# Weights of the first modulation loaded and summed by feature halves, the first slab of w_in ahead of them, ScalarE making the first four chunks

## The chip, the cores and the metric

One core of one Trainium2 chip. The time is device microseconds (us) of one execution of the whole program, the median of several runs. All times below that are not durations count from the start of the profiled span.

## The reference, cut to what matters

The program computes two transformer blocks on 512 tokens of 1024 features in float32. The change lies in the first 50 us, which compute the modulation and the first normalised, modulated input:

```python
mod = c @ w_ada[l] + b_ada[l]                 # c: (1, 1024), w_ada: (1024, 6144)
sh1, sc1, gt1, sh2, sc2, gt2 = jnp.split(mod, N_MOD, axis=-1)
h = modulate(rms_norm(x, g_pre_mix[l]), sh1, sc1)      # h * (1 + sc1) + sh1
proj = h @ w_in[l]                            # w_in: (1024, 5120)
```

All that follows (short convolution, stick-breaking attention, MLP, the second block) is untouched.

## The kernel before, in words

Features lie on the partitions: the 1024 features are 8 chunks (DC) of 128, the 512 tokens 4 row tiles (NT). A float32 product is made of three matmuls of split operands (`mm3`, L910 to L913): high part by high part, high by low, low by high. I call one such group of three a product of TensorE. Weights come as slabs of 2048 floats a partition (4 chunks by 512 columns, 1 MB) into a ring of three, `w_raw`. GpSimd splits each slab: `w_hi` (L757, for slab 0 L765), then `w_lo` = raw minus high (L759; for slab 0 four pieces, L769). The activations of chunk c are split too: ScalarE copies `ht_hi` (L1652, L1654), VectorE subtracts to `ht_lo` (L2202, recorded at L2050).

**The queue of SP.** All large loads go through one queue in the order of the program text: 16 blocks of w_ada (512 KB each, `ada`, L602, one chunk of 128 input features by the 1024 columns of shift for blocks 0 to 7 and of scale for 8 to 15), the four rows of x behind blocks 5, 7, 9 and 11 (X_WITH), then slab 0 of w_in, a wait for all 16 sums (L614), slab 1, slab 2, four blocks of w_ada for the next columns, and from there one slab and four blocks in turn. A block waits until the buffer of the block seven before it is free, a slab from slab 3 on until TensorE has begun the slab two before it (`slab_free`).

**VectorE** multiplies each block by a column of c and adds it to `ada_acc` (`ada_product`, L2144 on; recorded at L2059 for the first of a column and L2054 for the others). Between the products it makes the reciprocals of the row norms (NORM_WITH, L2072) and, behind block 11, copies the small vectors (VEC_WITH, L2183).

**TensorE** transposes each normalised row of x into six banks (`first_rows`, L1139), sums `ada_acc` over the partitions by matmuls with a column of ones (`first_sums`, L1113: for s = 0 the shift, for s = 1 the scale; a bank holds shift and scale of four chunks and is full after the fourth and eighth column of s = 1), transposes chunks 6 and 7 into the two banks that `first_mod` has emptied, and then starts `features`. For slab 0 this works by pieces: chunk `new` is awaited, and all products that it completes are done, 1 + 3 + 5 + 7 = 16 (L935 to L941).

**Behind the sums:** `first_mod` (VectorE, three operations of 4 columns a half), then pairs of chunks: VectorE scales and shifts the even chunk in PSUM (`first_affine`, L2061), ScalarE the odd one (L1650), ScalarE makes both high parts, VectorE both low parts. Then VectorE goes on with the products of the third and fourth column of w_ada, the convolution of the first branch, the fifth column, and the gating, whose results free banks and so let TensorE go on.

## Time and profile before

| | us |
|---|---|
| median of 3 runs (range) | 1486.69 (1484.39 to 1486.77) |
| the profiled execution | 1484.37 |
| its span | 1482.6 |
| TensorE matmul busy | 1440.1 |
| VectorE busy | 851.4 |
| GpSimd busy | 990.2 |
| ScalarE busy | 552.9 |

Durations and moments come from the one profiled execution; what lies around its span is 1.8 us. PE is TensorE's matmul, PEld its weight load, DVE VectorE, ACT ScalarE, POOL GpSimd, SP the engine that issues most DMAs (SPq its queue). Matmuls are pipelined, so that a row can show 0.39 us where the next matmul starts 0.23 us later. Where the profile shows a small operation x16, it can be eight float32 matmuls in two passes each.

### The profile page before, as it was taken

The page shows a single profiled execution, that of the slowest core. Times are in us where ns is not written, and L with a number is a line of the kernel's source. Part 1 is how long each engine was busy: PE and PEld are TensorE (multiplying, and loading weights), DVE is VectorE, ACT ScalarE, POOL GpSimd, SP SyncE. Part 2 cuts the span into 40 slices and gives each one's busy share as a digit, 9 for nine tenths or more (in the row PEclk, how much of TensorE's full clock was granted, in tenths as well). Part 3 has the DMA queues.
Part 4 walks back from the last instruction along what each step waited for, and adds up shares of the span by engine and source line. Part 5 has one row for each costly group of instructions (what it writes and reads, how often), then busy time and mean ns, then how long its engine had stood idle before and what let it go on. Part 6 is the DMA issues. An engine that isn't in the chain of part 4 may idle for free.

```text
span 1482.6 us, 18612 instructions
## 1 busy us (share of the span) xinstructions
PE 1440.1 (97%) x6987; PEld 1169.7 (79%) x6987; DVE 851.4 (57%) x1334; ACT 552.9 (37%) x1075; POOL 990.2 (67%) x400
## 2 busy tenths in 40 slices
PE   3999999999999999999999999999999999999997
PEld 3888877778898888888898844789789888888886
DVE  6998156554565555666744786441516555465655
ACT  3201133433454344444333376452424523333214
POOL 1857554355668899888568996365153989788653
PEclk9999999999999999999999999999999999999999
DMA  9875321223543332322443200133024323232131
GB/s 349 298 270 209 100 85 57 86 86 106 169 153 114 114 113 87 114 86 85 156 126 109 86 1 1 59 125 123 7 86 142 114 86 114 86 114 86 57 97 74
DMA packets 103385, 167.88 MB, mean 113 GB/s; under 512 B 3917, under 2 KB 61185, under 8 KB 102785
## 3 DMA queue, kind: packets, MB, share of 16 engines
q1 hardware_dynamic: 100176, 160.45, 31.7%
q10 hardware_dynamic: 3121, 6.26, 1.4%
q8 instruction: 56, 0.92, 0.2%
q14 instruction: 32, 0.26, 0.1%
HBM read 161.97 MB, written 4.72 MB: 112 GB/s over the span
## 4 chain that ended last, share of the span: by engine, by line
PE 84%; DVE 10%; ACT 3%; DMA 2%; issue 1%; POOL 1%; DVEq 0%; SPq 0%; ACTq 0%; POOLq 0%
PE bank L911 25%; PE bank L913 25%; PE bank L912 25%; DVE bank L2054 2%; DMA ada_w<-in_w_ada 1%; DVE smx L2507 1%; DVE x L2050 1%; PE bank L1372 1%; PE bank L1429 1%; PE bank L1448 1%; DVE bank L2050 1%; PE bank L1183 1%; DVE m L2050 1%; ACT junk L1541 1%; PE bank L1195 1%
## 5 line engine op out<-in xcount | busy, mean ns | idle before, releaser
L911 PE MATMUL bank<-ht_hi,w_hi 128*128 128x512 f32 (+1 forms) x1200 | 442.9, 369 | 0.5 <-DVE ht_lo L2050 0.3
L912 PE MATMUL bank<-ht_hi,w_lo 128*128 128x512 f32 (+1 forms) x1200 | 440.1, 367 | 0.0
L913 PE MATMUL bank<-ht_lo,w_hi 128*128 128x512 f32 (+1 forms) x1200 | 440.0, 367 | 0.0
L759 POOL TENSOR_TENSOR w_lo<-w_raw,w_hi 128x2048 fp32r<-128x2048 f32 x83 | 389.8, 4697 | 6.9
L757 POOL TENSOR_SCALAR w_hi<-w_raw 128x2048 fp32r<-128x2048 f32 x83 | 162.3, 1955 | 343.5 <-DMA w_raw<-in_w_in 111.2
L911 PEld LDWEIGHTS bank<-ht_hi,w_hi 128*128 128x128 f32 x1200 | 226.5, 189 | 41.6 <-issue 2.7
L913 PEld LDWEIGHTS bank<-ht_lo,w_hi 128*128 128x128 f32 x1200 | 226.6, 189 | 37.1
L912 PEld LDWEIGHTS bank<-ht_hi,w_lo 128*128 128x128 f32 x1200 | 226.6, 189 | 36.8 <-issue 0.5
L809 POOL TENSOR_TENSOR dn_lo<-dn_raw,dn_hi_all 128x1024 fp32r<-128x1024 f32 x77 | 184.6, 2418 | 56.7 <-ACT dn_hi_all L1738 56.6
L2054 DVE SCALAR_TENSOR_TENSOR uc<-bank,par,uc 128x511 f32<-128x511 f32 x88 | 66.0, 750 | 128.7 <-ACT uc L1992 125.6
L823 POOL TENSOR_TENSOR dn_raw<-dn_raw 128x1024 f32<-128x1024 f32 x44 | 105.8, 2404 | 12.8 <-PE bank L913 4.8
L911 PE MATMUL bank<-w_hi,ht_hi 128*128 128x512 f32 x256 | 100.4, 392 | 0.2 <-DVE facc L2050 0.2
L1992 ACT ACTIVATE uc<-bank,par 128x512 f32<-128x512 f32 x44 | 34.4, 781 | 176.9 <-PE bank L913 176.7
L913 PE MATMUL bank<-w_lo,ht_hi 128*128 128x512 f32 x256 | 99.7, 389 | 0.0
L912 PE MATMUL bank<-w_hi,ht_lo 128*128 128x512 f32 x256 | 99.6, 389 | 0.0
L2050 DVE TENSOR_TENSOR facc<-bank,facc 128x512 f32<-128x512 f32 x120 | 83.0, 692 | 22.4 <-PE bank L913 14.3
L2054 DVE SCALAR_TENSOR_TENSOR ada_acc<-ada_w,cvec,ada_acc 128x1024 f32<-128x1024 f32 x42 | 85.2, 2028 | 8.0 <-DMA ada_w<-in_w_ada 4.2
L1738 ACT CAST dn_hi_all<-dn_raw 128x1024 fp32r<-128x1024 f32 x77 | 77.1, 1054 | 18.4 <-PE bank L913 15.2
L2050 DVE TENSOR_TENSOR bank<-bank,hr 128x512 f32<-128x512 f32 x32 | 22.4, 700 | 82.9 <-ACT hr L1751 82.3
L911 PE MATMUL bank<-dn_hi_all,hf_hi 128*128 128x512 f32 x176 | 68.6, 390 | 0.4 <-POOL dn_lo L809 0.4
L912 PE MATMUL bank<-dn_hi_all,hf_lo 128*128 128x512 f32 x176 | 68.5, 389 | 0.0
L913 PE MATMUL bank<-dn_lo,hf_hi 128*128 128x512 f32 x176 | 68.5, 389 | 0.0
(305 smaller groups left out, 2415.7 us busy)
## 6 DMA issues: line engine op xcount, KB each, us to landing
w_raw<-in_w_in SPq DMA_DIRECT2D x27, 1024.0 KB, 5.0
ada_w<-in_w_ada SPq DMA_DIRECT2D x48, 512.0 KB, 7.3
w_raw<-in_w_up SPq DMA_DIRECT2D x22, 1024.0 KB, 5.0
w_raw<-in_w_mlp_in SPq DMA_DIRECT2D x16, 1024.0 KB, 5.5
dn_raw<-in_w_mlp_out SPq DMA_DIRECT2D x28, 512.0 KB, 4.8
w_raw<-in_w_out SPq DMA_DIRECT2D x8, 1024.0 KB, 5.0
w_raw<-in_w_mem_kv SPq DMA_DIRECT2D x8, 1024.0 KB, 5.2
dn_raw<-in_w_down SPq DMA_DIRECT2D x16, 512.0 KB, 4.7
```

Of the source, the lines that this page charges most:

```text
L757: g.tensor_scalar(w_hi[:, r], w_raw[:, r], 1.0, 1.0, ALU.mult, ALU.mult).then_inc(slab_hi, 1)
L759: g.tensor_tensor(w_lo[:, r], w_raw[:, r], w_hi[:, r].bitcast(F32), ALU.subtract).then_inc(slab_split, 1)
L809: g.tensor_tensor(dn_lo[:, w], dn_raw[:, w], dn_hi(w).bitcast(F32), ALU.subtract).then_inc(dn_split, 1)
L823: g.tensor_tensor(dn_raw[:, o], dn_raw[:, a], dn_raw[:, b], ALU.subtract).then_inc(t_made, 1)
L911: inc_free(pe.matmul(o, ah, bh, start=start, stop=False))
L912: pe.matmul(o, al, bh, start=False, stop=False)
L913: return pe.matmul(o, ah, bl, start=False, stop=stop)
L1183: ins = pe.transpose(t.ap[:, qt * P:qt * P + P], b1[:, j, O1[qt] + kc * P:O1[qt] + kc * P + P], ident[:])
L1738: st.done(act.copy(dn_hi(w), dn_raw[:, w]), dn_cast)
L1992: st.done(act.activation(uc[:, c], tiles[c].ap[:], ACT.Identity, scale=par[:, p, 2 + g, k:k + 1], bias=par[:, p, 6 + g, k:k + 1]), uc_ready)
L2050: do(v.tensor_tensor(o, a, b, op), sem, tile)
L2054: do(v.scalar_tensor_tensor(out=o, in0=a, scalar=s, in1=b, op0=op0, op1=op1), sem, tile)
```

## The change

The first 16 blocks of w_ada are cut otherwise. Block i below 8 now holds 512 columns of shift and the same 512 columns of scale (features 0 to 511) of input chunk i; blocks 8 to 15 hold the other 512 of both. So the first eight sums give shift and scale of chunks 0 to 3. Slab 0 goes ahead of all blocks, a row of x follows each of blocks 0 to 3, and the wait of the queue ahead of slab 1 is gone. The first sums are followed by slab 0's work at once; chunk 6's transposes, the second sums and chunk 7's transposes stand inside it (`within`). For chunks 0 to 3 ScalarE makes affine and high part alone; VectorE puts the products of blocks 8 to 15 around the first modulation and the low parts. Slab 1's high part is made by ScalarE, and its low part by GpSimd, behind a wait for all 16 sums.

```diff
@@ -43,9 +43,9 @@
 ADA_BUFS = 7
-X_WITH = (5, 7, 9, 11)
-NORM_WITH = (7, 9, 11, 13)
-VEC_WITH = 11
+X_WITH = (0, 1, 2, 3)
+NORM_WITH = (1, 2, 3, 4)
+VEC_WITH = 5
...
@@ -599,19 +599,23 @@
                 if i >= ADA_BUFS:
                     sp.wait_ge(ada_used, i - ADA_BUFS + 1)
                 s = i // DC
-                sp.dma_start(ada_w[:, r], wada[:, i % DC, s * D:(s + 1) * D]).then_inc(ada_loaded[r], 16)
-
+                if s < 2:
+                    sp.dma_start(ada_w[:, r].rearrange("p (j n) -> p j n", j=2),
+                                 wada[:, i % DC, 0:2 * D].rearrange("p (j n) -> p j n", j=2)[:, :, 512 * s:512 * s + 512]
+                                 ).then_inc(ada_loaded[r], 16)
+                else:
+                    sp.dma_start(ada_w[:, r], wada[:, i % DC, s * D:(s + 1) * D]).then_inc(ada_loaded[r], 16)
+
+            win = w_rows(A["w_in"])
+            load(raw4, win[:, 0:4, 512:1024])
             for i in range(2 * DC):
                 ada(i)
                 if i in X_WITH:
                     m = X_WITH.index(i)
                     sp.dma_start(x[:, m], A["x"][m * P:m * P + P, :]).then_inc(x_loaded[m], 16)
-            win = w_rows(A["w_in"])
             i = 2 * DC
             for c0 in (512, 1024, 0, 1536, 2048, 2560):
-                for s in range(2):
-                    if n == 1:
-                        sp.wait_ge(ada_used, 2 * DC)
+                for s in range(1 if c0 == 512 else 0, 2):
                     load(raw4, win[:, 4 * s:4 * s + 4, c0:c0 + 512])
                     for _ in range(4 if n > 2 else 0):
                         if i < 6 * DC:
@@ -755,13 +759,12 @@
                 g.wait_ge(slab_loaded[r], i * 16 + 16 * (n // RING + 1))
                 g.sem_inc(slab_go, 1)
                 g.tensor_scalar(w_hi[:, r], w_raw[:, r], 1.0, 1.0, ALU.mult, ALU.mult).then_inc(slab_hi, 1)
-                g.wait_ge(slab_hi, i * RING + n + 1 - (FF1_J - 2 if n >= S0["memkv2"] - 2 else 0))
+                g.wait_ge(slab_hi, i * RING + n - (FF1_J - 2 if n >= S0["memkv2"] - 2 else 0))
                 g.tensor_tensor(w_lo[:, r], w_raw[:, r], w_hi[:, r].bitcast(F32), ALU.subtract).then_inc(slab_split, 1)
 
             def split_first():
 
                 g.wait_ge(slab_loaded[0], 16)
-                g.wait_ge(ada_used, 2 * DC)
                 g.tensor_scalar(w_hi[:, 0], w_raw[:, 0], 1.0, 1.0, ALU.mult, ALU.mult).then_inc(slab_hi, 1)
                 g.wait_ge(slab_hi, 1)
                 raw, hi, lo = (w[:, 0].rearrange("p (k n) -> p k n", k=4) for w in (w_raw, w_hi, w_lo))
@@ -800,7 +803,9 @@
             taps = conv31()
             n = S0["w_in2"] + 6
             split_first()
-            split(1)
+            g.wait_ge(second_hi, 1)
+            g.wait_ge(ada_used, 2 * DC)
+            g.tensor_tensor(w_lo[:, 1], w_raw[:, 1], w_hi[:, 1].bitcast(F32), ALU.subtract).then_inc(slab_split, 1)
             split_all(2, S0["mlp"])
 
             def split_down(u, w):
...
@@ -936,7 +942,9 @@
                             each(new)
                             Tile(t0 + new).wait_free(pe)
                             pe.wait_ge(first_lo if new < 3 else slab_split, new + 1 if new < 3 else 1)
-                            for m, k in [(m, new) for m in range(new)] + [(new, k) for k in range(new + 1)]:
+                            for at, (m, k) in enumerate([(m, new) for m in range(new)] + [(new, k) for k in range(new + 1)]):
+                                if (new, at) in within:
+                                    within[new, at]()
                                 c = slice(m * P, m * P + P)
                                 mm3(Tile(t0 + m).ap[:, 0:n], wh[:, k, c], wl[:, k, c], ah[:, k], al[:, k], k == 0, False)
                         state["owed"] += 1
@@ -1106,13 +1114,13 @@
 
                 pe.wait_ge(ada_used, DC * (s + 1))
                 for c in range(DC):
-                    t = Tile(T0["ada01"] + c // 4)
-                    if s == 0 and c % 4 == 0:
+                    t = Tile(T0["ada01"] + s)
+                    if c == 0:
                         t.wait_free(pe)
-                    at = DC * s + c
+                    at = DC * (c // 4) + 4 * s + c % 4
                     ins = pe.matmul(t.ap[:, at:at + 1], ada_acc[:, s, c * P:c * P + P], ones[:, 0:1], start=True,
                                     stop=True)
-                    if s == 1 and c % 4 == 3:
+                    if c == DC - 1:
                         ins.then_inc(t.full, 1)
 
             def modulation(s):
@@ -1143,14 +1151,16 @@
             for m in range(NT):
                 if m == 1:
                     turn_rows()
-                if m == NT - 1:
-                    first_sums(0)
                 first_rows(range(DC - 2), m)
-            first_sums(1)
-            for c in (DC - 2, DC - 1):
+            first_sums(0)
+
+            def first_chunk(c):
                 for m in range(NT):
                     first_rows((c,), m)
-            features(T0["w_in"], 2, ht_hi, ht_lo, each=lambda k: Tile(NT1_T[k]).wait_taken(pe), first=True)
+
+            features(T0["w_in"], 2, ht_hi, ht_lo, each=lambda k: Tile(NT1_T[k]).wait_taken(pe), first=True,
+                     within={(1, 0): lambda: first_chunk(DC - 2), (3, 3): lambda: first_sums(1),
+                             (3, 6): lambda: first_chunk(DC - 1)})
             for c in range(1, 5):
                 features(T0["w_in"] + 4 * c, 2, ht_hi, ht_lo)
             tokens(T0["w_in"] + 20, 2, ht_hi, ht_lo)
@@ -1641,14 +1651,25 @@
                 norm_stat("nt1", m, x[:, m])
                 act.wait_ge(norm_inv, NB["nt1"] + m + 1)
                 st.done(act.activation(xn1[:, m], x[:, m], ACT.Copy, scale=stat[:, 16 + m:17 + m]), xn_ready)
-            for pair in range(DC // 2):
+            def first_affine(c):
+                t = Tile(NT1_T[c])
+                t.wait_full(act)
+                st.done(act.activation(t.ap[:], t.ap[:], ACT.Identity, scale=mod[:, 1, c:c + 1], bias=mod[:, 0, c:c + 1]))
+
+            Tile(T0["ada01"]).wait_taken(act)
+            for c in range(4):
+                first_affine(c)
+                act.wait_ge(act_step, st.value(act_step))
+                st.done(act.copy(ht_hi[:, c], Tile(NT1_T[c]).ap[:]), nt1_hi)
+            act.wait_ge(slab_loaded[1], 16)
+            st.done(act.copy(w_hi[:, 1], w_raw[:, 1]), second_hi)
+            for pair in range(DC // 4, DC // 2):
                 c = 2 * pair + 1
                 if pair % 2 == 0:
                     Tile(T0["ada01"] + pair // 2).wait_taken(act)
                 t = Tile(NT1_T[c])
-                t.wait_full(act)
-                st.done(act.activation(t.ap[:], t.ap[:], ACT.Identity, scale=mod[:, 1, c:c + 1], bias=mod[:, 0, c:c + 1]))
-                act.wait_ge(nt1_affine, pair + 1)
+                first_affine(c)
+                act.wait_ge(nt1_affine, pair - DC // 4 + 1)
                 st.done(act.copy(ht_hi[:, c - 1], Tile(NT1_T[c - 1]).ap[:]), nt1_hi)
                 act.wait_ge(act_step, st.value(act_step))
                 st.done(act.copy(ht_hi[:, c], t.ap[:]), nt1_hi)
@@ -2172,7 +2193,7 @@
                         if j % 2:
                             stt(mod[:, j], mod[:, j], 1.0, col((V_G1, V_GM1)[j // 2], 8), ALU.add, ALU.mult)
 
-            for i in range(2 * DC):
+            for i in range(DC):
                 ada_product(i)
                 if i in NORM_WITH:
                     norm_inv_of("nt1", NORM_WITH.index(i))
@@ -2201,13 +2222,17 @@
                 v.wait_ge(nt1_hi, c + 1)
                 tt(ht_lo[:, c], t.ap[:], ht_hi[:, c].bitcast(F32), ALU.subtract, tile=t)
 
+            for i in range(DC, DC + 2):
+                ada_product(i)
             first_mod(0)
-            first_affine(0)
+            for c in range(4):
+                ada_product(DC + 2 + c)
+                first_low(c)
+            for i in range(DC + 6, 2 * DC):
+                ada_product(i)
             first_mod(1)
-            first_low(0)
-            first_affine(2)
-            first_low(1)
-            for pair in range(1, DC // 2):
+            first_affine(4)
+            for pair in range(2, DC // 2):
                 if pair + 1 < DC // 2:
                     first_affine(2 * pair + 2)
                 first_low(2 * pair)
```

## Rows read from the trace of the kernel before

**Rows 1.** The page, parts 1 and 2: busy time; granted clock in 40 slices

```profile
PE 1440.1 (97%) x6987; PEld 1169.7 (79%) x6987; DVE 851.4 (57%) x1334; ACT 552.9 (37%) x1075; POOL 990.2 (67%) x400
...
PEclk9999999999999999999999999999999999999999
```

**Rows 2.** List of waits of PE, whole run: total us, times, longest

```profile
PE bank L1139 <- ACT xn L1643: 19.9, 3, 15.7
...
PE bank L1183 <- DVE b L2050: 3.2, 1, 3.2
```

**Rows 3.** Timeline, DVE, 0 to 34: start, us, operation, idle before

```profile
4.37 0.75 DVE L2059 TENSOR_SCALAR ada_acc<-ada_w,cvec 128x1024 f32<-128x1024 f32 x1 [0.95 <-DMA ada_w<-in_w_ada]
...
14.68 1.28 DVE L2054 SCALAR_TENSOR_TENSOR ada_acc<-ada_w,cvec,ada_acc 128x1024 f32<-128x1024 f32 x1 [1.56 <-DMA ada_w<-in_w_ada]
...
19.21 0.75 DVE L2059 TENSOR_SCALAR ada_acc<-ada_w,cvec 128x1024 f32<-128x1024 f32 x1 [1.51 <-DMA ada_w<-in_w_ada]
...
22.76 2.67 DVE L2054 SCALAR_TENSOR_TENSOR ada_acc<-ada_w,cvec,ada_acc 128x1024 f32<-128x1024 f32 x2 [0.90 <-DMA ada_w<-in_w_ada]
...
25.80 0.60 DVE L2183 COPY vec<-bank 128x428 f32<-128x428 f32 x1
...
29.77 2.67 DVE L2054 SCALAR_TENSOR_TENSOR ada_acc<-ada_w,cvec,ada_acc 128x1024 f32<-128x1024 f32 x2
```

**Rows 4.** Timeline, PE, 30 to 51

```profile
32.86 3.41 PE L1113 MATMUL bank<-ones,ada_acc 128*128 128x1 f32 x16
...
36.13 1.97 PE L1139 MATMUL bank<-ident,xn 128*128 128x128 f32 x8
...
37.77 0.77 PE L911 MATMUL bank<-ht_hi,w_hi 128*128 128x512 f32 x1
...
39.49 0.77 PE L911 MATMUL bank<-ht_hi,w_hi 128*128 128x512 f32 x1
...
50.17 0.39 PE L911 MATMUL bank<-ht_hi,w_hi 128*128 128x512 f32 x1
```

**Rows 5.** Timeline, POOL, 30 to 60

```profile
32.77 1.90 POOL L765 TENSOR_SCALAR w_hi<-w_raw 128x2048 fp32r<-128x2048 f32 x1 [30.24 <-DMA w_raw<-in_w_in]
...
34.75 4.98 POOL L769 TENSOR_TENSOR w_lo<-w_raw,w_hi 128x512 fp32r<-128x512 f32 x4
...
41.69 4.62 POOL L759 TENSOR_TENSOR w_lo<-w_raw,w_hi 128x2048 fp32r<-128x2048 f32 x1
...
55.79 1.92 POOL L757 TENSOR_SCALAR w_hi<-w_raw 128x2048 fp32r<-128x2048 f32 x1 [2.59 <-DMA w_raw<-in_w_in]
```

**Rows 6.** Busy time by stretches: engines, clock, share of DMA, GB/s

```profile
15.00:20.00 5.00, 1.06 (x5) 1.07 (x6) 3.17 (x4) 2.17 (x3) 0.00 (x0) 1.00 1.03 405
...
35.00:40.00 5.00, 4.89 (x18) 3.87 (x19) 3.75 (x9) 3.85 (x7) 5.00 (x5) 1.00 1.05 412
```

**Rows 7.** Timeline, ACT, 12 to 36

```profile
13.19 1.06 ACT L1541 ACTIVATE junk<-x 128x1024 bf16<-128x1024 f32 x1 [4.06 <-DMA x<-in_x]
...
14.37 0.29 ACT L1543 ACTIVATE stat<-stat,eps_t 128x1 f32<-128x1 f32 x1
...
17.74 1.15 ACT L1643 ACTIVATE xn<-x,stat 128x1024 f32<-128x1024 f32 x1 [3.07 <-DVE stat L2065]
...
35.20 0.75 ACT L1650 ACTIVATE bank<-bank,mod 128x512 f32<-128x512 f32 x1 [4.35 <-DVE mod L2050]
```

**Rows 8.** Timeline, DVE, 46 to 55

```profile
46.56 2.19 DVE L2059 TENSOR_SCALAR ada_acc<-ada_w,cvec 128x1024 f32<-128x1024 f32 x1
...
48.85 5.43 DVE L2054 SCALAR_TENSOR_TENSOR ada_acc<-ada_w,cvec,ada_acc 128x1024 f32<-128x1024 f32 x1
```

**Rows 9.** Timeline, PE, around 171

```profile
171.56 3.63 PE L1129 MATMUL bank<-ones,ada_acc 128*128 128x1 f32 x32
```

**Rows 10.** Timeline, SP and POOL, 106 to 123: slab 8

```profile
106.76 0.43 SPq L588 DMA_DIRECT2D w_raw<-in_w_in  x1
...
116.55 5.46 POOL L759 TENSOR_TENSOR w_lo<-w_raw,w_hi 128x2048 fp32r<-128x2048 f32 x1
```

More of the change, by code:

```diff
@@ L455, in build @@
         slab_hi, slab_split, slab_free = sem("slab_hi"), sem("slab_split"), sem("slab_free")
-        slab_go, first_lo = sem("slab_go"), sem("first_lo")
+        slab_go, first_lo, second_hi = sem("slab_go"), sem("first_lo"), sem("second_hi")
         c_loaded, rows_loaded, mem_loaded = sem("c_loaded"), sem("rows_loaded"), sem("mem_loaded")
@@ L920, in all_taken, with features @@
                     Tile(t).wait_taken(pe)
-            def features(t0, ks, ah, al, i=None, tper=0, sper=0, n=T, each=None, first=False, behind=None):
+            def features(t0, ks, ah, al, i=None, tper=0, sper=0, n=T, each=None, first=False, behind=None,
+                         within={}):
                 for s in range(ks):
```

## The prediction

> **What bounds the kernel now.** The page comes first: TensorE is busy 97% of the span and nothing else is over 80% [rows 1]. The list of PE waits over the whole run says where the other 3% lies: 19.9 us wait for the normalised rows at the very start, and the next wait is 3.2 us [rows 2]. So whatever lets TensorE enter its dense part earlier comes off the end one for one, as long as nobody is late behind it. The timeline of the first 51 us is where the change is decided. VectorE sums sixteen 512 KB blocks of w_ada as they land, the last ending at 29.77 + 2.67 = 32.44 [rows 3]; TensorE turns the sums (until 36.3), and its first weight product starts at 37.77 [rows 4]. The sixteen products of slab 0 (three matmuls each) end at 50.17, where slab 1 begins [rows 4]. I call 50.17 the entry: from there TensorE runs at 0.68 us a product, 10.9 us a slab. The sum below is the new entry against 50.17.
>
> **When the first half is summed.** The queue now carries slab 0, then a block of w_ada and a row of x in turn, then blocks only. Counting places of 512 KB, the rows tell when a place is usable: place 1 at 4.37, 8 at 14.68, 11 at 19.21, 14 at 22.76 [rows 3], slab 0 (places 21 and 22) at 32.77 [rows 5]. The new order puts slab 0 at 5.8, block 0 (place 3) at 7.2, block 1 at 10.2, 2 at 13.2, 3 at 16.2, 4 at 19.2, 5 at 20.4, 6 at 21.6, 7 (place 14) at 22.8. The new w_ada blocks consist of 2 KB runs instead of 4 KB. The trace has both kinds: 405 GB/s in 15:20 with 4 KB runs, 412 GB/s in 35:40 with the slabs' 2 KB runs [rows 6]. I charge nothing.
>
> VectorE also makes four reciprocals and the copy of vec. A row of x costs ScalarE 1.47 (13.19 to 14.66) for the deviation, then 0.2 for the reciprocal and 1.15 for the scaling [rows 7], about 3.0 a row. From x at 8.8 the reciprocals fall at 11.7, 14.7, 17.7 and 20.7, each within 0.4 us behind a product that is ready; so product 5 runs 20.9 to 22.2, vec and mod_g take 0.9 (25.80 to 26.7 [rows 3]), product 7 ends at 25.8, two at 1.34 each. The data alone would allow 24.1.
>
> GpSimd's split of slab 0 moves from 32.77 to 5.8, beside products 0 and 1; it takes 1.9 + 4.98 in four pieces [rows 5]. A product that takes 1.28 alone [rows 3] took 5.43 beside a 2048-wide w_lo [rows 8], so a piece of 1.25 can hold one by at most its own length: 0 to 1.3, twice at most. I take 0.5: first half summed at 26.3. The Trainium skill (SBUF — State Buffer, Who interferes with whom) says that a VectorE instruction with two SBUF inputs and a GpSimd one that reads SBUF exclude each other for a whole instruction. The 5.43 agrees with it; by the rule product 1 waits for one piece, a delay between 0 and 1.25, which would not change the forecast.
>
> **When TensorE starts.** Before, 5.33 us passed from the last product to the first matmul (32.44 to 37.77). The chain is kept (sums, three small VectorE operations, affine 0.75 [rows 7], copy, difference), but the first tile is now full after all eight columns instead of four of the second eight: half of 3.41, +1.7 [rows 4]. ScalarE did the odd chunks' affines before, at 0.75 [rows 7], as fast as VectorE, so its doing chunk 0's costs nothing. Start: 26.3 + 5.3 + 1.7 = 33.3, which is 4.4 earlier.
>
> **What TensorE now does behind the start.** Slab 0 took 12.4 from start to entry and needs it again. New inside it:
> - The second half's sums. The same sixteen instructions took 3.41 at the start [rows 4], but 32 of them took 3.63 at 171 us [rows 9], so 1.8 if TensorE runs at its full pace by then. It has twelve products behind it: I take 1.8.
> - The transposes of chunks 6 and 7, before ahead of the start: 1.97 for eight at the slow pace [rows 4], about 1.05 at the fast one. I take 1.5.
> - VectorE puts a product (1.34) between two differences (0.7), so chunk 1 is ready 2.1 behind the start, where the first product took 1.6: 0.5.
> - The slow pace at the start (first product 1.6, second 1.16, then 0.68) lasts a little longer with that pause and the transposes in it: 0 to 3 (six products at 1.16), I take 0.5.
> - The second half's chunks: from the end of its sums, modulation 0.8, two affines 1.8, copies and four differences take about 6.0 until chunk 7 is taken; TensorE has four products, chunk 7's transposes and three products of slab 1 to do, 5.4. A wait of 0.5.
>
> VectorE reaches product 15 at about 42.4 (30.9, six products, four differences), ahead of TensorE's twelfth product at 44.5, so the sums don't wait. Slab 1's w_lo waits behind it on GpSimd, to 47: ahead of the entry. ScalarE's w_hi of slab 1 (about 2, twice its 1024-wide operations) falls into its idle time around 37. Entry: 33.3 + 12.4 + 1.8 + 1.5 + 0.5 + 0.5 + 0.5 = 50.5, against 50.2: **0.3 us later**. The head start of 4.4 is spent on 4.8 of work that formerly stood before the start or lay in waits.
>
> **Behind the entry.** VectorE starts the third column's products at about 52.8 instead of 46.56. But before, its first two took 7.7 us, to 54.3, beside slab 2's split (2.19 and 5.43 [rows 8]); now that split passes beside operations that read PSUM, and the two take 2.2, to 55.0. The next must begin before slab 3's w_hi (55.79 [rows 5]); it does by 0.8. If not, VectorE is a product behind until a w_lo of 5.46 [rows 10] falls on the last of the fourth column, and everything behind it is up to 5.5 late. There is cover: slab 8 is issued at 106.76, held back by product 32, and split at 122.0 [rows 10]; TensorE wants it at 50.2 + 7 x 10.88 = 126.3. The cover is 4.3, so this costs 0 to 1.2. On SP, slab 1 and 2 no longer wait for the sixteenth sum (32.4) and nothing stands behind that wait.
>
> **The time.** The profiled execution took 1484.37 for a span of 1482.6; with +0.3 it is 1484.7. The median of the runs is 1486.69, 2.3 above that execution, so the forecast is 1487.0.
>
> **Rivals.**
> 1. *The head start is kept.* If VectorE follows the data (24.1 instead of 26.3) and TensorE is fast from its second product, the entry is 50.5 - 2.2 - 1.0 - 0.5 = 46.8, or 3.4 earlier: 1483.3. For it: the reciprocals lag by only tenths each. Against it: ScalarE's 3.0 a row is as long as two places of the queue, so there is no slack to catch up.
> 2. *TensorE stays at its slow pace through slab 0.* The first matmuls took 0.77 where later ones take 0.39, though the granted clock stands at 1.00 throughout, the 2.4 GHz level [rows 1, 4]. The slow stretch followed a stretch of transposes and one-column sums. If the pause behind chunk 0 and chunk 6's transposes extend it by six products (+3.0, less the 0.5 counted) and the sums fall into it (+1.6), with the transposes at 2.0 (+0.5), the entry is 4.6 later than mine, 4.9 later than before: 1491.6. It decides from about five slow products on (+2.7 over before). For it: TensorE now has gaps in just this stretch. Against: before, it was fast 2.9 us behind 37.77. The Trainium skill (TensorE: Matmul & The Clock Gate, What you observe) says that the clock doubles only after sustained matmuls; by it the first products run at 1.2 GHz. The durations agree, the granted-clock column doesn't show it, and the price above is from rows.
> 3. *VectorE slips a product behind.* Condition and price above: +0.3 and up to 1.2, 1488.2. Near a coin's edge (0.8 us), but within what is told apart.
> 4. *The change does nothing*: were the entry set by slab 1's split. It isn't: slab 1 was split at 46.3 before [rows 5], 3.9 ahead.
>
> **Chances.** Forecast 0.44, rival 3 0.16, rival 1 0.20, rival 2 0.16, others 0.04. A measurement here tells 0.2% (3.0 us) from no change. Forecast and rival 3 lie within it; rival 1 is just beyond it, and half of the rest goes to either side: faster 0.22, same 0.60, slower 0.18. The range goes from 1482.8 (a little beyond rival 1, for 0.5 less delay by GpSimd) to 1490.5 (rival 2 with four slow products instead of six).
>
> **What would show it.** First weight product at 33.3 (32 to 34.5); slab 1's first matmul at 50 to 51; product 7 ending near 26; the second sums at half their old duration; PE wait of some 0.5 in front of chunk 6 or 7 of slab 1; product 18 starting ahead of slab 3's w_hi; no PE wait near 126. A first product after 35.5 or an entry before 48 would prove me wrong.

## The result, and the profile after

The changed kernel takes 1487.88 us (median of 22 runs, 1486.13 to 1493.65); the kernel before, on the same chips, 1485.24 (22 runs). The ratio is 1.0021, 95% interval [1.0013, 1.0028]: 3.1 us slower, 1.9 to 4.2. The profiled execution of the changed kernel took 1493.65 and is one of its longest (four of the 22 lie above 1491.8, the others between 1486 and 1490); experiment 12 has the profile of an execution near the usual time.

The page after, and the list of PE waits over the whole run (columns as in [rows 1] and [rows 2]):

```profile
PE 1442.8 (97%) x6987; PEld 1168.7 (78%) x6987; DVE 846.6 (57%) x1332; ACT 555.7 (37%) x1078; POOL 986.6 (66%) x399
```

```profile
PE bank L1147 <- ACT xn L1653: 12.0, 3, 10.4
PE bank L916 <- DVE yt_lo L2071: 6.4, 1, 6.4
...
PE bank L1193 <- DVE b L2071: 3.3, 1, 3.3
```

The start did what it was to do: the wait for the normalised rows fell from 19.9 to 12.0. In its place stands a wait of 6.4 for yt_lo, which the kernel before doesn't have. The timeline of VectorE, as [rows 3, 8]:

```profile
23.76 2.67 DVE L2075 SCALAR_TENSOR_TENSOR ada_acc<-ada_w,cvec,ada_acc 128x1024 f32<-128x1024 f32 x2
...
51.80 2.23 DVE L2080 TENSOR_SCALAR ada_acc<-ada_w,cvec 128x1024 f32<-128x1024 f32 x1
54.12 4.06 DVE L2075 SCALAR_TENSOR_TENSOR ada_acc<-ada_w,cvec,ada_acc 128x1024 f32<-128x1024 f32 x3
61.35 7.44 DVE L2075 SCALAR_TENSOR_TENSOR ada_acc<-ada_w,cvec,ada_acc 128x1024 f32<-128x1024 f32 x2 [3.17 <-DMA ada_w<-in_w_ada]
...
99.33 0.70 DVE L2071 TENSOR_TENSOR bank<-bank,cv 128x512 f32<-128x512 f32 x1
...
112.91 15.49 DVE L2075 SCALAR_TENSOR_TENSOR ada_acc<-ada_w,cvec,ada_acc 128x1024 f32<-128x1024 f32 x7
...
131.72 2.28 DVE L2071 TENSOR_TENSOR yt_lo<-bank,yt_hi 128x512 fp32r<-128x512 f32 x3
```

The kernel before has at the same places:

```profile
91.89 0.70 DVE L2050 TENSOR_TENSOR bank<-bank,cv 128x512 f32<-128x512 f32 x1
...
106.46 11.07 DVE L2054 SCALAR_TENSOR_TENSOR ada_acc<-ada_w,cvec,ada_acc 128x1024 f32<-128x1024 f32 x7
...
120.86 3.08 DVE L2050 TENSOR_TENSOR yt_lo<-bank,yt_hi 128x512 fp32r<-128x512 f32 x4
```

The timeline of PE, as [rows 4]:

```profile
26.48 3.58 PE L1121 MATMUL bank<-ones,ada_acc 128*128 128x1 f32 x16 [2.36 <-DVE ada_acc L2075]
32.94 0.77 PE L916 MATMUL bank<-ht_hi,w_hi 128*128 128x512 f32 x1 [2.88 <-DVE ht_lo L2071]
...
35.13 1.09 PE L1147 MATMUL bank<-ident,xn 128*128 128x128 f32 x4 [0.56 <-DVE ht_lo L2071]
...
43.78 1.84 PE L1121 MATMUL bank<-ones,ada_acc 128*128 128x1 f32 x16
...
47.66 0.60 PE L1147 MATMUL bank<-ident,xn 128*128 128x128 f32 x4
...
49.45 0.47 PE L916 MATMUL bank<-ht_hi,w_hi 128*128 128x512 f32 x1 [0.49 <-DVE ht_lo L2071]
```

The product that starts at 49.45 is slab 1's first: 0.7 ahead of 50.17 [rows 4] (0.35 ahead by the end of slab 1's first tile, read from the first copy of cv: 52.74 after, 53.09 before). So up to here the change is neutral or a little better. Now ScalarE's own DMA queue, SP's issue of slabs 3 and 8, and GpSimd, as [rows 5, 10]:

```profile
49.38 0.36 ACTq L1541 DMA_DIRECT2D ada_b<-in_b_ada  x1
...
49.77 0.45 ACTq L1678 DMA_DIRECT2D gpost<-in_g_post_mix  x1
50.25 0.45 ACTq L1678 DMA_DIRECT2D gpost<-in_g_post_mlp  x1
```

```profile
49.95 0.38 SPq L588 DMA_DIRECT2D w_raw<-in_w_in  x1
...
113.21 0.43 SPq L588 DMA_DIRECT2D w_raw<-in_w_in  x1
```

```profile
60.26 1.91 POOL L761 TENSOR_SCALAR w_hi<-w_raw 128x2048 fp32r<-128x2048 f32 x1 [6.79 <-DMA w_raw<-in_w_in]
...
119.90 1.93 POOL L761 TENSOR_SCALAR w_hi<-w_raw 128x2048 fp32r<-128x2048 f32 x1 [14.22 <-DMA w_raw<-in_w_in]
121.91 5.42 POOL L763 TENSOR_TENSOR w_lo<-w_raw,w_hi 128x2048 fp32r<-128x2048 f32 x1
```

Slab 3 of the kernel before, for comparison, from SP's timeline (its w_hi is in [rows 5]):

```profile
50.59 0.38 SPq L588 DMA_DIRECT2D w_raw<-in_w_in  x1
```

ScalarE issues three loads of 512 KB (ada_b, gpost twice) behind its last copy of chunk 7. Before, they went out at 43.31 to 44.18 and had landed when slab 3 was asked for; now they go out at 49.38 to 50.25, around slab 3 (49.95). Slab 3 is usable 10.3 us behind its issue, before 5.2 (50.59 to 55.79), and the blocks behind it are late too: VectorE idles 3.17 for block 20. VectorE reaches the gating of the convolution at 99.33, before at 91.89: 7.4 late. Product 32 then comes 7.4 late as well, slab 8 is issued at 113.21 instead of 106.76 [rows 10], and one of the seven products behind it is caught by slab 8's w_lo (15.49 for seven; before 11.07). The end of this chain in TensorE's window (columns as in [rows 6]) and in ScalarE's timeline:

```profile
125.00:140.00 15.00, 8.59 (x33) 6.67 (x32) 13.64 (x14) 4.30 (x8) 9.60 (x3) 0.77 0.59 212
```

```profile
147.89 0.59 ACT L1645 COPY k<-bank 128x512 f32<-128x512 f32 x1 [13.70 <-PE bank L918]
```

And before:

```profile
125.00:140.00 15.00, 15.00 (x68) 12.43 (x67) 14.37 (x7) 0.59 (x1) 10.47 (x3) 1.00 0.42 129
```

```profile
140.13 0.59 ACT L1635 COPY k<-bank 128x512 f32<-128x512 f32 x1 [13.01 <-PE bank L913]
```

TensorE is busy 8.59 of 15 us where it was busy all 15 before, and the granted clock averages 0.77 (before 1.00). The first copy of k was at 140.13 before: 7.8 of the 9.3 us by which this span is longer are lost here, the other 1.5 at 180:190, where the clock stands at 0.84 and 0.82.

### The profile page after: what moved, and what is told of

Read it like the earlier page. It is cut to its first block, busy times and chain, and to the rows that moved or that the text cites. A ratio compares the mean times of both kernels' runs of the same rounds, so it can differ in the third digit from the quotient of the medians.

```text
span 1491.9 us, 18610 instructions
## 1 busy us (share of the span) xinstructions
PE 1442.8 (97%) x6987; PEld 1168.7 (78%) x6987; DVE 846.6 (57%) x1332; ACT 555.7 (37%) x1078; POOL 986.6 (66%) x399
## 4 chain that ended last, share of the span: by engine, by line
PE 79%; DVE 14%; ACT 3%; DMA 1%; issue 1%; DVEq 0%; SPq 0%; ACTq 0%
PE bank L916 24%; PE bank L917 23%; PE bank L918 23%; DVE ada_acc L2075 4%; DVE bank L2075 2%; DMA ada_w<-in_w_ada 1%; DVE bank L2071 1%; DVE smx L2532 1%; DVE x L2071 1%; PE bank L1382 1%; PE bank L1439 1%; PE bank L1458 1%; ACT junk L1551 1%; DVE m L2071 1%; PE bank L1205 1%
## 5 line engine op out<-in xcount | busy, mean ns | idle before, releaser
L763 POOL TENSOR_TENSOR w_lo<-w_raw,w_hi 128x2048 fp32r<-128x2048 f32 x82 | 382.6, 4665 | 6.8
```

What stands on the lines that cost most here:

```text
L763: g.tensor_tensor(w_lo[:, r], w_raw[:, r], w_hi[:, r].bitcast(F32), ALU.subtract).then_inc(slab_split, 1)
```

## Experiments

Each ran on one chip together with the kernel before, whose median there was 1484.65 for experiments 1 to 4, 1484.63 for 5 to 8, 1486.42 for 9 to 11 and 1484.27 for 12. The ratio is always to this kernel before. Median against median says less here than the ratio and the profile, since the kernel before itself has two levels, about 1484 and about 1487 (see experiments 5 and 9). A profile shows one execution, and where that is not a usual one the text says so.

**1. ScalarE's three loads early (in the changed kernel).**

```
     st.done(act.copy(w_hi[:, 1], w_raw[:, 1]), second_hi)
+    load_ada_b(0, 2)
+    for j, name in enumerate(("g_post_mix", "g_post_mlp")): act.dma_start(gpost[:, j], ...)
...  # behind chunk 7's copy:
-    load_ada_b(0, 2)
-    for j, name in ...
```

> The changed kernel, with ScalarE's three 512 KB loads (ada_b, two of gpost) issued behind its copy of slab 1's high part, near 38, instead of behind chunk 7, at 49.4 to 50.3. Theory 1 (collision): in the changed kernel these loads stood in the DMA engines together with slab 3 and blocks 20 to 23 (slab 3 took 10.3 us from issue to use instead of 5.2), and that alone put VectorE behind; with them gone the wait for yt_lo (6.4) falls to nothing, slab 8 is issued near 107, and the time is 0.3 to 0.8 us under the kernel before (ratio 0.9995 to 1.0). Theory 2 (late start): VectorE begins the third column 5.2 us later than before (51.8 against 46.56), and that puts it behind whatever the DMA does; then the wait stays at 4 us or more and the ratio at 1.002.

1486.41 (12 runs), ratio to before 1.0002 [0.9993, 1.0011]. GpSimd's and VectorE's timelines:

```profile
55.04 2.08 POOL L761 TENSOR_SCALAR w_hi<-w_raw 128x2048 fp32r<-128x2048 f32 x1 [1.64 <-DMA w_raw<-in_w_in]
```

```profile
51.77 2.19 DVE L2080 TENSOR_SCALAR ada_acc<-ada_w,cvec 128x1024 f32<-128x1024 f32 x1
54.06 20.86 DVE L2075 SCALAR_TENSOR_TENSOR ada_acc<-ada_w,cvec,ada_acc 128x1024 f32<-128x1024 f32 x7
...
96.98 0.70 DVE L2071 TENSOR_TENSOR bank<-bank,cv 128x512 f32<-128x512 f32 x1
```

The loads went out at 35.42 to 36.29. Slab 3 is usable 5.1 behind its issue (49.92) again, the wait for yt_lo is gone, and k is copied at 140.11. With this one edit the ratio falls from 1.0021 to 1.0002: the loss came from where the loads went. The profile is of the shortest of the 12 executions (1484.04). VectorE is still 5.1 late at the convolution (96.98), and slab 8 is issued at 110.86, 4.1 late: that costs nothing.

**2. The kernel before, its loads held back.** The same meeting made without any of the change.

```
+    act.wait_ge(slab_free, 1)      # TensorE has left slab 0
     load_ada_b(0, 2)
```

> The kernel before, with ScalarE waiting until TensorE has begun slab 1 (slab_free at 1, near 50.3) before it issues the same three loads. Theory 1: slab 3 lands some 4 to 5 us later, VectorE waits for block 20, reaches the convolution some 5 us late, and the first yt_lo comes behind the moment at which TensorE wants its bank (126): a PE wait of 1 to 6 us and a ratio of 1.0007 to 1.004. Theory 2: VectorE starts on time, so the third column has the same lead as before; no PE wait near 126 and a ratio of 1.000.

1488.09 (11 runs), ratio 1.0015 [1.0006, 1.0024]. Its PE waits and GpSimd's timeline:

```profile
PE bank L911 <- DVE yt_lo L2051: 6.4, 1, 6.4
```

```profile
60.07 1.92 POOL L757 TENSOR_SCALAR w_hi<-w_raw 128x2048 fp32r<-128x2048 f32 x1 [7.21 <-DMA w_raw<-in_w_in]
```

One wait in the old kernel reproduces the late slab (issued 50.79, usable 60.07), and in the profiled execution the wait of 6.4 and the late k copy (148.71) too. That execution is the longest of the 11 (1492.94, the others 1486.56 to 1488.88), so the wait of 6.4 is shown for it alone; the loss of the others is seen in the ratio. With experiment 1 this shows the cause from both sides.

**3. Slab 0 behind block 7 (on top of experiment 1).**

```
-    load(raw4, win[:, 0:4, 512:1024])      # ahead of block 0
+    if i == 7: load(raw4, win[:, 0:4, 512:1024])
```

> The first kernel of this series (loads early) with slab 0 behind block 7 in the queue instead of ahead of block 0. Everything up to the first half's sums comes two places (2.7 us) earlier: product 7 ends near 23.8 instead of 26.4, the first weight product starts near 30.3 instead of 32.9, slab 1's first matmul near 47 instead of 49.4, since VectorE's products 8 to 15 also move. Slab 0's split then lies beside products 7 to 9. If the head start is spent inside slab 0 whatever it is, as TensorE's own work, this gives 2 to 2.7 us against the first kernel of the series: ratio to before near 0.998. If the data of blocks 8 to 15 (same place as before) bound the second half, it gives under 1 us.

1486.96 (12 runs), ratio 1.0015 [1.0002, 1.0028]. VectorE's timeline:

```profile
19.75 0.16 DVE L2087 RECIPROCAL stat<-stat 128x1 f32<-128x1 f32 x1 [1.40 <-ACT stat L1554]
...
22.33 4.11 DVE L2076 SCALAR_TENSOR_TENSOR ada_acc<-ada_w,cvec,ada_acc 128x1024 f32<-128x1024 f32 x2
```

The blocks came earlier and nothing else did: VectorE waited 1.40 for ScalarE at each of the last three reciprocals, which are 2.95 apart (a row of x is ScalarE's bound), and products 6 and 7 took 4.11 instead of 2.67 beside slab 0's split. Product 7 ended at 26.44, as before the edit (26.37), and slab 1 began at 50.63, 1.2 later than in experiment 1 (49.42). The expectation that all would come 2.7 sooner fell.

**4. The gating ahead of three products of the fifth column (in the changed kernel).**

```
-    ada_products(4)
+    for c in range(5): ada_product(4 * DC + c)
     ...gating, yt_lo...
+    for c in range(5, DC): ada_product(4 * DC + c)
```

> The changed kernel, with VectorE doing the gating and yt_lo behind five products of the fifth column instead of behind all eight (the other three follow). If the bank that yt_lo frees is what TensorE waits for, the wait of 6.4 goes; what is late next is slab 8, issued at 113.2 and split at 127.3 against TensorE's 125.7, so 1.6 to 2 us of wait remain: 4 to 5 us less than the changed kernel where that one waits 6.4, and in the median a ratio of 1.000 to 1.0015. If it was slab 8 that TensorE waited for, nothing changes.

1492.12 (5 runs), ratio 1.0042 [1.0028, 1.0056]: worse, where 1.000 to 1.0015 had been expected. Its PE waits:

```profile
PE bank L916 <- POOL w_lo L763: 3.8, 1, 3.8
```

VectorE makes yt_lo from 121.53 on and k is copied at 140.37, so this wait can be moved away. But SP issues slab 10 only behind blocks that wait for those products: at 137.12, and TensorE waits 3.8 for its split. Behind this wait the granted clock stands at 0.87 and 0.79 over 150:160, so that more than the 3.8 is lost. It is the same lateness of VectorE, paid at its next customer.

**5. VectorE's order at the start (on top of 1).** From experiment 3: the fourth reciprocal and the copy of vec stand in front of products whose blocks are there.

```
-NORM_WITH = (1, 2, 3, 4); VEC_WITH = 5
+NORM_WITH = (1, 2, 3, 5); VEC_WITH = 7
```

> The changed kernel with ScalarE's three loads early (as in the first experiment) and VectorE's order at the start altered: the fourth reciprocal behind product 5 instead of product 4, and the copy of vec with mod_g behind product 7 instead of product 5. Theory A (the entry is set by VectorE's chain up to product 7, and the rest of the start follows it one for one): product 7 ends at 24.3 instead of 26.43 (it starts when its block has landed, about 23.0), first weight product at 30.8 instead of 32.9, slab 1's first matmul at 47.3 instead of 49.4, third column of VectorE at 49.7, no PE wait for yt_lo, k copy of the fifth column at 137.3 to 138; time 2.8 us below the kernel before. Theory B (the head start is spent again before the entry, on TensorE's slow first products and on waits for the second half's chunks): first weight product at 30.8, but slab 1's first matmul at 48.5 or later; time within 1.5 us of the kernel before. Theory C (the reciprocal put back delays ScalarE's last row so that its transposes hold the sums): first weight product not before 32.

1484.87 (11 runs), ratio 0.9995 [0.9987, 1.0004]. VectorE:

```profile
21.75 2.67 DVE L2075 SCALAR_TENSOR_TENSOR ada_acc<-ada_w,cvec,ada_acc 128x1024 f32<-128x1024 f32 x2
...
50.45 1.55 DVE L2080 TENSOR_SCALAR ada_acc<-ada_w,cvec 128x1024 f32<-128x1024 f32 x1
...
90.75 0.70 DVE L2071 TENSOR_TENSOR bank<-bank,cv 128x512 f32<-128x512 f32 x1
```

Product 7 ends at 24.42, the first weight product starts at 30.93, slab 1 at 48.10, the first k copy stands at 138.47: 1.7 ahead of before (the entry is 0.8 later than theory A had it: from start to entry 17.2 us passed, in the changed kernel 16.5; one cause is that the second and third product ran at the slow pace longer, full pace from 36.29, 5.4 behind the start, instead of 4.0). VectorE starts its third column 1.3 earlier than in experiment 1 and reaches the convolution 6.2 earlier: one product fewer is caught by a w_lo. Yet the span is 1482.8. The 1.7 is gone again, while the waits behind 146 us are those of the kernel before within 0.3 us each. The window rows (columns as in [rows 6]) tell:

```profile
170.00:175.00 5.00, 5.00 (x34) 4.69 (x33) 2.54 (x6) 0.00 (x0) 0.00 (x0) 0.75 0.27 104
175.00:180.00 5.00, 5.00 (x11) 2.83 (x10) 2.95 (x7) 0.00 (x0) 0.00 (x0) 0.57 0.09 19
```

TensorE counts as busy, but at a granted clock of 0.57. This begins within the 32 one-column sums (here 4.45, [rows 9] 3.63), and the stretch from SP's issue of slab 12 (the first of w_proj_conv, 146.85) to that of slab 14 (178.43) takes 31.6 where it takes 28.8 in the kernel before (148.51 to 177.28). That is a loss of 2.8, more than the 1.7. The rest comes back further on: the kernel before has a fall of its own at 225:235 (0.81 and 0.85), where TensorE has just waited 3.2 for VectorE's b (a tile of the attention); here the clock stays at 1.00 there, and from slab 14 to the next slab, issued near 291, it takes 112.8 instead of 113.7.

**6. The second sums behind 10 products instead of 12 (on top of 5).**

```
-within={..., (3, 3): first_sums(1), (3, 6): first_chunk(DC - 1)}
+within={..., (3, 1): first_sums(1), (3, 4): first_chunk(DC - 1)}
```

> The kernel before this one, and TensorE's second sums behind 10 of slab 0's 16 products instead of 12, chunk 7's transposes behind 13 instead of 15. Theory A: VectorE's product 15 ends ahead of the tenth product, so nobody waits for the sums; chunks 6 and 7 are ready 1.4 us earlier, the 0.5 us wait at slab 1 goes, VectorE's third column starts another 1.4 us earlier (48.3); time 0.5 us below the kernel before this one, 3.3 below the kernel before the change. Theory B: TensorE reaches the sums ahead of product 15 and waits 0.5 to 1.3 us, and the time is the same as without this edit or up to 1 us worse.

1484.45 (12 runs, three of them above 1488), ratio 0.9998 [0.9985, 1.0010]. The wait of 0.5 in front of slab 1 is gone, as theory A had it, but the profiled execution (1488.84, one of the three) lost 4.2 at yt_lo:

```profile
109.53 0.43 SPq L588 DMA_DIRECT2D w_raw<-in_w_in  x1
```

```profile
PE bank L916 <- DVE yt_lo L2071: 4.2, 1, 4.2
```

Slab 8 is issued 4.1 later than in experiment 5 (105.39) though VectorE started its third column 0.4 sooner (50.01): its first product was caught for 2.51 instead of 1.55 beside slab 2's split, and a product more fell behind a w_lo later. Neither theory had named this; it is the prediction's rival 3.

**7. The low parts of chunks 0 and 1 without a product between (on top of 6).** The edit: VectorE's product DC + 3 goes behind first_low(1) instead of in front of it.

> As the kernel before this one, and VectorE makes the low parts of chunks 0 and 1 one behind the other, with no product between. Theory A: TensorE's wait of 0.57 in front of chunk 1 goes and its products come to full pace sooner; slab 1's first matmul 0.5 earlier; product 15 at most 0.5 later, still ahead of the sums; time 0.5 us lower. Theory B: product 15 comes later than the tenth product, TensorE waits for the sums what it saved at chunk 1: no difference.

1484.81 (11 runs), ratio 0.9997 [0.9988, 1.0006]. Slab 1 starts at 47.17, 0.9 before experiment 5's and 3.0 before the old kernel's; the product is caught again (slab 8 issued at 109.56), TensorE waits 1.4 for slab 8's w_lo, and k is copied at 138.78. Then the clock falls to 0.57 in 175:180. Three us of head start brought nothing to the end.

**8. Experiment 6 with the loads where the change put them.**

> As e7 (start order and sums), but ScalarE's three loads stay behind its copy of chunk 7, where the change put them. The collision theory: the loads and slab 3 both move forward by about 2.5 us and still meet; slab 3's high part 9 to 11 us behind its issue instead of 5.2, VectorE waits 3 us or more for block 20 or its neighbours; but VectorE starts some 3 us earlier than in the changed kernel, so conv begins at 96 to 97, yt_lo comes in time, and the time is within 0.7 us of e7 in most executions. The rival (the meeting costs its 4 to 6 us whenever it happens, since VectorE's order has no slack anywhere): PE waits 3 to 6 us for yt_lo and the time is 2 us or more above e7.

1485.48 (12 runs, six at 1483.0 to 1483.9 and six at 1487.1 to 1494.6), ratio 1.0009 [0.9993, 1.0026]. The profile is of a short one (1482.0): slab 3, issued at 48.09, is usable at 57.03 (8.9 later), slab 8 is issued at 110.07, k copied at 139.29. So it is as the collision theory had it for half of the executions; the other half lies 4 to 11 us higher, and none of it was profiled.

**9. The kernel before, its sums taken apart.** The 32 one-column sums are 16 of column 3 and 16 of column 4; the four wide ones of column 2 go between.

```
-for s in range(2, 6): modulation(s)
+for s in (3, 2, 4, 5): modulation(s)
```

> The kernel before the change with one edit: behind the last column of the first stage TensorE makes the sums of w_ada in the order 3, 2, 4, 5 instead of 2, 3, 4, 5, so that its 32 one-column matmuls (3.6 us) are no longer in one piece but 16 and 16 with four wide ones (1.9 us) between. Theory D (the two levels in which the times of every kernel here lie, some 1484 and some 1487, are a drop of TensorE's granted clock behind these 32 sums: in the profiles of three kernels it stood at 0.57 in one 5 us window at 175:180 or 180:185 or near it and the stretch from slab 11 to slab 12 took 31.6 to 31.9 us, in the others at 1.00 and 28.8): with the sums apart nearly every execution is at 1484, the median falls to 1484.0 or below and none is above 1486. Rival D2 (the levels come from elsewhere, or it is not the sums' length that decides): the two levels stay with the same shares, median 1484.6 as before.

1484.05 (11 runs, 1482.98 to 1485.01) against 1486.42 for the kernel before on the same chip (29 runs, 18 of them above 1485.9): ratio 0.9985 [0.9977, 0.9994]. The upper level is gone. PE's timeline and the window:

```profile
169.90 1.84 PE L1129 MATMUL bank<-ones,ada_acc 128*128 128x1 f32 x16
171.60 1.96 PE L1126 MATMUL bank<-ada_acc,ones 128*128 128x512 f32 x4
173.40 1.84 PE L1129 MATMUL bank<-ones,ada_acc 128*128 128x1 f32 x16
```

```profile
175.00:180.00 5.00, 5.00 (x21) 3.52 (x21) 1.77 (x5) 0.17 (x1) 0.00 (x0) 1.00 0.59 189
```

So the upper level of the old kernel goes with the sums in this order. That it is the clock is argued and not seen in this kernel: its one profile is of the lower level, and the drop of 2.8 us in the profile of experiment 5 is about the distance of the levels. The mean granted clocks fit: 0.9975 over the 62 executions of the old kernel below 1485.2 in these series, 0.9962 over the 46 above. Whether it is the gap between the sums or only their order was not told apart.

**10. Experiment 5 with the sums apart.**

> The changed kernel with ScalarE's loads early, the start order of VectorE (fourth reciprocal behind product 5, vec behind product 7) and the sums apart as in the kernel above. Theory D and theory A of the start together: TensorE is 1.7 us ahead of the kernel before at the k copies, as measured without the sums apart (138.47 against 140.13), and the 2.8 us that the clock's drop then took at 170:180 are not lost: nearly every execution at 1482.5 to 1483.2, median 1483.0, 1.6 below the kernel before. Rival: the drop comes all the same, median 1484.5 to 1485 as without the edit.

1482.37 (12 runs, 1481.24 to 1484.65), ratio 0.9979 [0.9971, 0.9988]: 3.1 us faster than the kernel before (1.8 to 4.3), and the best version of this study. On that chip the kernel before was mostly at its upper level. Against experiment 9, which has the sums apart too, 1.7 of median remain for the early start. The profile (1484.40) is of one of the two longest executions: k is copied at 139.23, 0.9 ahead of the kernel before, and slab 14 is issued 0.9 ahead too (176.38), but at 225:235 the clock stands at 0.51 and 0.80, behind the wait of 3.2 for b, and by the next slab, issued near 291, the lead is gone.

**11. Experiment 10 and the low parts together.**

> As the kernel above, and VectorE makes the low parts of chunks 0 and 1 with no product between. Theory A: the wait in front of chunk 1 (0.57) goes, slab 1's first matmul 0.5 us earlier, and TensorE reaches its k copies at 137.9; median 1482.5. Rival 3 of the prediction (a product of VectorE slips behind a w_lo of GpSimd): VectorE's first products of the third column, started at another time beside slab 3's split, put one product beside a w_lo more; slab 8 is issued at 109.5 instead of 105.4, and TensorE waits 1 to 4 us at yt_lo or slab 9; median 1484 or more.

1482.86 (12 runs: nine below 1484.3, three at 1487.8 to 1489.5), ratio 0.9987 [0.9973, 1.0000]. Slab 8 was issued at 109.75 instead of 106.00: the product is caught again, as rival 3 had it, but in this profile (1484.27) TensorE didn't wait for it, and k is copied at 139.05, against 139.23 in experiment 10. The time of 1484 or more that rival 3 named was found in a third of the executions, three of them at 1487.8 or more.

**12. The changed kernel with the sums apart.** The edit is that of experiment 9.

> The changed kernel with one edit: the sums of w_ada in the order 3, 2, 4, 5, so that TensorE's 32 one-column matmuls are in two pieces. It tells which of the two losses the changed kernel's usual execution holds (22 executions, none below 1486.1, most at 1487 to 1488.6, some at 1492), since its profile shows only one of the longest. If it is the meeting of ScalarE's loads with slab 3 and the wait for yt_lo alone: the times stay near 1486 to 1488 and the profile shows a wait of TensorE for yt_lo or for a w_lo. If the clock's drop behind the sums makes the usual 1487 (so that the meeting of the loads costs only the executions at 1492): the lowest are at 1483.5 to 1484.5, the median at 1485 or below. If both have a share: lowest near 1484, median 1486, some at 1490.

1487.21 (11 runs, 1485.78 to 1493.79), ratio 1.0026 [1.0014, 1.0037]. By the expectation this is the first case: dividing the sums doesn't take the changed kernel's loss away (1487.88 with them undivided, on other chips), so the clock behind them has a small share at most. This profile (1486.49) is of one of three executions just below the median. GpSimd, VectorE and PE:

```profile
60.48 1.92 POOL L761 TENSOR_SCALAR w_hi<-w_raw 128x2048 fp32r<-128x2048 f32 x1 [7.11 <-DMA w_raw<-in_w_in]
...
123.04 5.43 POOL L763 TENSOR_TENSOR w_lo<-w_raw,w_hi 128x2048 fp32r<-128x2048 f32 x1
```

```profile
112.95 11.08 DVE L2075 SCALAR_TENSOR_TENSOR ada_acc<-ada_w,cvec,ada_acc 128x1024 f32<-128x1024 f32 x7
...
127.34 3.08 DVE L2071 TENSOR_TENSOR yt_lo<-bank,yt_hi 128x512 fp32r<-128x512 f32 x4
```

```profile
128.52 0.50 PE L916 MATMUL bank<-ht_hi,w_hi 128*128 128x512 f32 x1 [1.69 <-POOL w_lo L763]
```

VectorE and slab 8 (issued at 113.24) are as late as in the profile above; only the eighth product escapes slab 8's w_lo. yt_lo's first piece ends at 128.0, ahead of that w_lo (128.5). TensorE waits 1.7 for the w_lo, k is copied at 142.45, 2.3 later than before, and the span is 2.2 longer. Of the 2.3, 0.3 were there at the first copy of cv already (53.40 against 53.09). From the convolution to slab 8's split these two profiles differ by this one product.

## Why the prediction came out right, and where it was wrong

The forecast was 1487.0 and the result 1487.88. The number is right within 0.9 us, the change is not: 0.3 us were forecast and 3.1 measured (1.9 to 4.2), at the edge of what was called no change. That the two numbers agree is luck: the forecast stood on the median of three runs of the kernel before (1486.69), two of which lay in its upper level; over 22 runs that median is 1485.24.

- *First half summed*: 26.3 forecast, 26.43 measured. Right. Products 0 to 2 took 1.25, 1.95 and 2.29 beside slab 0's split. The 0.5 charged for that wasn't paid, for VectorE waited for its blocks or for ScalarE behind each of them; the reciprocals (the fourth at 21.18 instead of 20.7) took its place.
- *Start of TensorE*: 33.3 forecast, 32.94 measured. Right.
- *Between start and entry*: second sums 1.8 (1.84), wait at chunk 1 0.5 (0.56), transposes 1.5 (1.1: 0.74 and 0.36 from their start to the next matmul), a longer slow pace 0.5 (nothing: the second product took 1.11, before 1.16), wait in front of slab 1 0.5 (0.49). Entry 50.5 forecast, 49.45 measured. The head start was spent here as forecast, save 0.7. Rival 2 (a slow TensorE through slab 0) did not happen in this profile: full pace from the third product on, at 36.98. A small form of it exists: in the profile of experiment 12 the granted clock is 0.50 over 25:35 and 0.70 over 35:40, the third product is slow too, and the entry is at 50.10. The mean clock of that execution is 0.993, and five of the 22 of the changed kernel lie at 0.991 to 0.993, of 108 of the kernel before none (0.995 or more).
- *Rival 1* (the head start is kept) did not happen either; experiment 5 shows what it would have taken. VectorE's order held product 7 back: it stood waiting 1.07 for ScalarE's fourth row with block 5 there to be summed, and 2.0 of the 2.2 named there were had by the order alone. So the argument that ScalarE's 3.0 a row leaves no slack (2.95 measured) held only for the order as it was. Even so the entry came at 48.10, not at the rival's 46.8.
- *Behind the entry*: **this step failed.** It took slab 3's w_hi as still at 55.79; it came at 60.26. The prediction had followed SP's queue past the entry but not ScalarE's: ScalarE's three loads stand behind chunk 7's copy, which the change moved by 6 us onto slab 3's issue. The sum has no term for them. Of the signs that the prediction named, "no PE wait near 126" failed by this (6.4 in the profile above, 1.7 in that of experiment 12).
- *Rival 3* had the right mechanism. It asked whether product 18 begins ahead of slab 3's w_hi. With the loads early it didn't quite (experiment 1: two products took it to 55.3, w_hi came at 55.04), VectorE became 5.1 late ("up to 5.5"), slab 8 4.1 late, and the cover of 4.3 took it all: cost 0, within the 0 to 1.2 of the price. In the changed kernel the collision adds 2.3, slab 8 is 6.5 late, and 6.5 - 4.3 = 2.2. Experiment 12 measured a wait of 1.7, since TensorE came to slab 8 only at 126.8 instead of 126.3. So the cover was sized about right; what was put against it was not. What the prediction had not priced is the second customer of VectorE's lateness, yt_lo: where a w_lo catches one product more, TensorE waits 6.4.
- *The chances*: rival 3 was given 0.16 with 1488.2. A price for the loads' meeting would have raised both.

The Trainium skill (DMA: Bandwidth & Descriptors, Queues, rings and completion order) says that a DMA engine takes turns, packet by packet, between the queues that have work for it. The trace is in keeping with it, though it doesn't show the turns themselves: slab 3 took 10.3 instead of 5.2 us with 1.5 MB of another queue in flight. The Trainium skill (SBUF — State Buffer, Who interferes with whom) says that a VectorE instruction with two SBUF inputs and a GpSimd one that reads SBUF shut each other out for a whole instruction. The products that took up to 5.45 us instead of 1.28 beside a w_lo of 5.46 agree with it.

What stays open: which small shifts decide, from one execution to the next, whether a product is caught by a w_lo. The profiles show that it happens (experiments 6, 7 and 11), not what shifts the engines by tenths. Open too is what the executions with a mean clock of 0.990 to 0.993 cost: experiment 1 has five of them among 12, at 1486.40 to 1487.82, while its lowest five are at 1484.04 to 1485.00 (0.997 or 0.998), and none of the five was profiled.

## What to carry to other kernels

When a step is moved on an engine, list every DMA that this engine issues behind it and lay their new times over the other queues': here three loads that are first read behind 170 us cost about 3 us, and issuing them 14 us earlier took that back. An engine far off the critical path (VectorE, 57% busy) needs its lateness followed to each of its customers, with the cover of each as a number; moving work away from one (experiment 4) only finds the next. And if gained time vanishes with no wait in the list, look at the granted clock by windows before looking for a dependency.

## What the runs showed of the hardware

- TensorE's granted clock fell though TensorE hadn't just waited. Behind 32 one-column matmuls (3.6 us, counted as busy) it fell in seven of the ten profiles with the sums in one piece, for example to 0.57 over 175:180 in experiments 5 and 7 and to 0.66 over 180:185 in 4 and 6; in the kernel before and experiments 1 and 8 it stayed at 1.00. In two pieces of 16 with wide matmuls between it stayed at 1.00 over 165:190 in all four profiles (experiments 9 to 12), and the kernel before lost its upper level of times. The fall cost 2.8 us in experiment 5.
- Dividing the sums removes that fall and no other: in the same four profiles the clock fell at 225:235, behind a wait of 3.2 to 3.3 us for b, to between 0.50 and 0.92 in the first 5 us. In experiment 5, behind a wait of 3.35, it stayed at 1.00, and the 16 transposes behind the wait took 1.94 us; in experiment 10, at 0.51, they took 3.65.
- Behind the wait of 6.4 us the clock stood at 0.50 over 130:135. From the first copy of cv to the first copy of k 8.1 us were lost against the kernel before (7.8 at the copy of k, and the lead of 0.35 at that of cv). Behind the wait of 1.7 it stood at 1.00, and 2.0 were lost on the same stretch.
- Two queues share the DMA engines, and a transfer isn't served ahead of one that is issued later on the other queue: in experiment 2 slab 3 was issued together with the first of ScalarE's three 512 KB loads and ahead of the other two (50.79 against 50.79, 51.22 and 51.78), and was usable 9.3 us later instead of 5.2. In the changed kernel, issued 0.6 us behind the first of the loads, it was usable 10.3 later.
